# Stage seams of a two-layer encoder trunk worked by pairs of token tiles

## What is computed

```python
mod = (c_act @ w_ada[l] + b_ada[l])[:, None, :]
sh_a, sc_a, g_a, sh_m, sc_m, g_m = jnp.split(mod, 6, axis=-1)
h = x * (1.0 + sc_a) + sh_a
proj = h @ w_in[l]                      # heads of three attention mixers -> y
x = layer_norm(ALPHA * x + (1.0 + g_a) * (y @ w_o[l]), ln1_g[l], ln1_b[l])
h = x * (1.0 + sc_m) + sh_m
y = jnp.square(jax.nn.relu(h @ w1[l])) @ w2[l]
x = layer_norm(ALPHA * x + (1.0 + g_m) * y, ln2_g[l], ln2_b[l])
```

## Time and profile before

| | |
|---|---|
| median of three executions | 1447.26 us |
| the profiled execution | 1448.38 us |
| its span, first to last instruction | 1446.6 us |
| TensorE matmul busy | 1324.9 us (92%) |
| VectorE / ScalarE / GpSimd busy | 1011.6 / 598.5 / 339.9 us |
| granted TensorE clock, mean | 0.968 |
| DMA, mean | 114 GB/s |

### The profile page before, as it was taken

How to read it: one execution, slowest core, us unless ns; L and a number is a source line. 1 busy time by engine, 2 the same in 40 slices (tenths; PEclk the granted TensorE clock), 3 DMA queues, 4 the chain that set the end, 5 groups by cost and what they waited for, 6 DMA issues and landing times.

```text
span 1446.6 us, 19841 instructions
## 1 busy us (share of the span) xinstructions
PE 1324.9 (92%) x6696; PEld 1120.0 (77%) x6696; DVE 1011.6 (70%) x1650; ACT 598.5 (41%) x1212; POOL 339.9 (23%) x409
## 2 busy tenths in 40 slices
PE   4998998899899999999969899879989999999992
PEld 2897877787788888888869877768778888888882
DVE  6768788877678465565785878978674855454478
ACT  0356478851432222222244647878152232222221
POOL 0022066630125000000321406856010700000024
PEclk9999989999999999999989999999999999999996
DMA  8864600005233343344246462010423333333331
GB/s 284 302 203 165 204 14 14 27 22 173 76 119 128 117 129 113 100 129 147 79 154 202 155 212 72 1 39 1 145 87 96 95 99 97 94 98 98 95 102 58
DMA packets 87577, 164.38 MB, mean 114 GB/s; under 512 B 7960, under 2 KB 18584, under 8 KB 87504
## 3 DMA queue, kind: packets, MB, share of 16 engines
q1 hardware_dynamic: 86976, 161.34, 34.4%
q10 hardware_dynamic: 528, 2.10, 0.4%
HBM read 159.21 MB, written 4.19 MB: 113 GB/s over the span
## 4 chain that ended last, share of the span: by engine, by line
PE 68%; DVE 17%; DMA 6%; ACT 4%; issue 3%; POOL 2%; SPq 0%; ACTq 0%; DVEq 0%; POOLq 0%
PE bank L1325 21%; PE bank L1326 21%; PE bank L1327 21%; DMA ada_w<-in_w_ada 2%; DVE pt_lo L1076 2%; PE bank L1354 2%; DVE ada_sum L839 2%; PE bank L1492 2%; DMA slab_raw<-in_w_in 1%; DVE smax L1063 1%; DVE X L1104 1%; DVE stats L1107 1%; DVE tmp L1101 1%; DVE k_lo L1037 1%; DVE acc L1246 1%
## 5 line engine op out<-in xcount | busy, mean ns | idle before, releaser
L1325 PE MATMUL bank<-hT_hi,slab_hi 128*128 128x512 f32 x576 | 224.5, 390 | 1.2 <-ACT kB L658 1.2
L1156 DVE TENSOR_TENSOR slab_lo<-slab_raw,slab_hi 128x512 fp32r<-128x512 f32 x240 | 183.0, 815 | 60.1 <-ACT slab_hi L793 51.8
L1327 PE MATMUL bank<-hT_hi,slab_lo 128*128 128x512 f32 x576 | 224.1, 389 | 0.0
L1326 PE MATMUL bank<-hT_lo,slab_hi 128*128 128x512 f32 x576 | 224.1, 389 | 0.0
L1325 PE MATMUL bank<-slab_hi,h_hi 128*128 128x512 f32 x512 | 200.1, 391 | 2.8 <-ACT mod_a L810 2.8
L1327 PE MATMUL bank<-slab_hi,h_lo 128*128 128x512 f32 x512 | 199.3, 389 | 0.0
L1326 PE MATMUL bank<-slab_lo,h_hi 128*128 128x512 f32 x512 | 199.2, 389 | 0.0
L1325 PE MATMUL bank<-slab_hi,hT_hi 128*128 128x384 f32 (+3 forms) x448 | 151.6, 338 | 4.0 <-DVE hT_lo L1084 2.8
L1327 PE MATMUL bank<-slab_hi,hT_lo 128*128 128x384 f32 (+3 forms) x448 | 150.9, 337 | 0.0
L1326 PE MATMUL bank<-slab_lo,hT_hi 128*128 128x384 f32 (+3 forms) x448 | 150.8, 337 | 0.0
L839 DVE SCALAR_TENSOR_TENSOR ada_sum<-ada_w,c_col,ada_sum 128x512 f32<-128x512 f32 x168 | 129.5, 771 | 16.2 <-DMA ada_w<-in_w_ada 13.1
(11 more groups left out here) (198 smaller groups left out, 2601.2 us busy)
## 6 DMA issues: line engine op xcount, KB each, us to landing
slab_raw<-in_w SPq DMA_DIRECT2D x256, 256.0 KB, 2.7
ada_w<-in_w_ada SPq DMA_DIRECT2D x48, 1024.0 KB, 5.4
slab_raw<-in_w_in SPq DMA_DIRECT2D x48, 192.0 KB, 5.3
slab_raw<-in_w_o SPq DMA_DIRECT2D x32, 256.0 KB, 2.9
slab_raw<-in_w_in SPq DMA_DIRECT2D x16, 256.0 KB, 5.3
band<-bias_rows SPq DMA_DIRECT2D x8, 448.0 KB, 3.2
slab_raw<-in_w_in SPq DMA_DIRECT2D x16, 144.0 KB, 3.7
X<-in_x SPq DMA_DIRECT2D x1, 2048.0 KB, 10.1
```

The source lines that it names most:

```text
L1156: dve.tensor_tensor(slab_lo[:, slot, :], slab_raw[:, slot, :], f32(slab_hi[:, slot, :]), ALU.subtract).then_inc(slab_lo_done, 1)
L1325: pe.matmul(dst, a_hi, w_hi, start=first, stop=False)
L1326: pe.matmul(dst, a_hi, w_lo, start=False, stop=False)
L1327: return pe.matmul(dst, a_lo, w_hi, start=False, stop=last)
```

## The change

Tokens are handled in pairs of tiles, p = 0 (tiles 0, 1) and p = 1 (tiles 2, 3), at each seam.

- *Jobs and banks.* ln0 to ln3 become lnp, lnq (entry of a layer, pair 0 and 1) and lnr, lns (before the MLP). Each has eight pieces of 256 tokens, two to a bank. Banks come from a table (`SETS`, `EVEN`, `ODD`).
- *TensorE.* `wo_second` runs wo1 for pair 0, then pair 1, with pair 0's 16 transposes after slab 5 of pair 1. `first_group` runs W1's first group in two halves of 256 tokens, with pair 1's transposes around slab 7 of the first. `first_chunk` does the same for the first projection chunk. `last_group` leaves the W2 product of group 7 in the banks of group 6, pair 0 and then pair 1, and in layer 0 puts the next layer's first transposes between its slabs; in layer 1 tiles 2 and 3 come one after the other.
- *ScalarE* no longer normalises X. It evicts each piece once (256 tokens, `pair_tmp`), and VectorE casts and subtracts from that (`ht_low`).
- *GpSimd* normalises X with one subtract-and-multiply a half tile (`normalise`), so `shift` goes. It no longer takes part in the residual of the MLP.
- *VectorE.* `norm_exit` interleaves the residuals of tiles 2 and 3 with casts and splits. The gate and X are applied to `acc` (eight scalings, eight additions) before the squares of group 7; group 6 has no addition into `acc`.
- *Modulation.* The gate blocks 10 and 11 move to MLP groups 0 and 1 of each layer (`LATE`), a whole block a group; the next layer's blocks 0 to 3 are done in groups 2 to 5. "ad3" goes.
- *Output.* Eight stores of half tiles; GpSimd writes tiles 0 and 1, VectorE 2 and 3 (`last_affine`).
- *Memory.* Some SBUF tensors change their offsets; X, hT and the area of reused tensors start at multiples of 1024 bytes.

```diff
-        ("wo0", 0, 4), ("wo1", 0, 4), ("ad3", 2, 0), ("ln2", 4, 0), ("ln3", 4, 0), ("w1", 4, 0)]
+        ("wo0", 0, 4), ("wo1", 0, 4), ("lnr", 8, 0), ("lns", 8, 0), ("w1", 4, 0)]
...
+                def normalise(n):
+
+                    for t in range(TT):
+                        rstd_of(n, t)
+                        pool.wait_ge(rstd_ready, l * 8 + 4 * n + t + 1)
+                        for j in range(2):
+                            xs = X[:, t, 512 * j:512 * j + 512]
+                            pool.tensor_scalar(xs, xs, mv[:, t, MV_MEAN:MV_MEAN + 1], mv[:, t, MV_RSTD:MV_RSTD + 1],
+                                               ALU.subtract, ALU.mult).then_inc(xhat_ready, 1)
...
+                def ln_evac(job, which, k, l=l):
+                    p = int(job in ("lnq", "lns"))
+                    act.wait_ge(bank_ready, l * B_LAYER + ready_before(job) + k // 2 * 2 + 2)
...
+                    if 8 * p + k >= 4:
+                        act.wait_ge(ht_ready, l * 32 + which * 16 + 8 * p + k - 3)
+                    act.activation(pair_tmp(k), ln_bank(job, k), ACT.Identity, **move).then_inc(evac_act, 1)
+
+                def norm_entry(job, which, first, width, l=l):
+                    for k in range(4):
+                        split(first + k, width, l)
+                    ln_evac(job, which, 0, l)
+                    for k in range(4):
+                        ln_evac(job, which, k + 1, l)
+                        split(first + 4 + k, width, l)
+                    for k in range(5, 8):
+                        ln_evac(job, which, k, l)
...
+                def ht_low(job, k, l=l):
+                    p = int(job in ("lnq", "lns"))
+                    dve.wait_ge(evac_act, l * A_LAYER + a_before(job) + k + 1)
+                    step(dve.tensor_copy(hT_hi[:, k, pair_cols(p)], pair_tmp(k)))
+                    settle()
+                    dve.tensor_tensor(hT_lo[:, k, pair_cols(p)], pair_tmp(k), f32(hT_hi[:, k, pair_cols(p)]),
+                                      ALU.subtract).then_inc(ht_ready, 1)
...
+                def norm_exit(n, job, first, width, src, half_done, all_done, l_next):
+                    ht_low(job, 0, l_next)
+                    ht_low(job, 1, l_next)
+                    half_done()
+                    at2 = take(src(2), n, 2, 1)
+                    all_done()
+                    at3 = take(src(3), n, 3, 1)
+                    split(first + 4, width, l_next)
+                    ht_low(job, 2, l_next)
+                    add_to_x(n, 2, 1, at2)
+                    split(first + 5, width, l_next)
+                    stats_of(2, 1)
+                    add_to_x(n, 3, 1, at3)
+                    ht_low(job, 3, l_next)
+                    stats_of(3, 1)
+                    moments(2)
+                    split(first + 6, width, l_next)
+                    moments(3)
+                    ht_low(job, 4, l_next)
+                    split(first + 7, width, l_next)
+                    for k in range(5, 8):
+                        ht_low(job, k, l_next)
...
+                def first_group():
+                    def columns(p, ks, cs):
+                        for k in ks:
+                            pe.wait_ge(ht_ready, l * 32 + 16 + 8 * p + k + 1)
...
+                    columns(0, range(3), (0, 1))
+                    pe.wait_ge(evac_dve, l * D_LAYER + d_before("wo1") + 4)
+                    columns(0, range(3), (2, 3))
+                    columns(0, range(3, 7), range(4))
+                    transpose_x("lns", 1, range(4))
+                    columns(0, range(7, 8), range(4))
+                    transpose_x("lns", 1, range(4, 8))
+                    columns(1, range(8), range(4))
...
+                for j in range(2):
+                    for f in range(4):
+                        last_group((0, 1), j, f)
+                if l < DEPTH - 1:
+                    for f in range(4):
+                        last_group((2, 3), 0, f)
+                    for f in range(4):
+                        last_group((2, 3), 1, f)
+                        if f == 1:
+                            pe.wait_ge(evac_dve, l * D_LAYER + D_LAST + 4)
+                            transpose_x("lnp", 0, range(8), l + 1)
```

More of the change, by code:

```diff
@@ L490, in _ @@
                         affine_part(t, part, lnrow[:, 0, :], lnrow[:, 1, :])
[L492 to L510, removed]
@@ new lines, in _, with scale_acc @@
+                for k in range(4):
+                    split_at(k, base_at + (PRE + 16 + k + 1))
+                dve.wait_ge(x_ready, l * 8 + 8)
+                dve.wait_ge(evac_act, relu_base + 5 * LATE)
+                dve.wait_ge(evac_dve, l * D_LAYER + D_LAST)
+                gated[0] = D_LAST
+                def scale_acc(t, j):
+                    a = acc[:, t, 512 * j:512 * j + 512]
+                    step(dve.tensor_tensor(a, a, gate[:, 1, 512 * j:512 * j + 512], ALU.mult))
+                    return now()
@@ new lines, in base_of_x @@
+                def base_of_x(t, j, at):
+                    xs = X[:, t, 512 * j:512 * j + 512]
+                    dve.wait_ge(dve_step, at)
+                    step(dve.scalar_tensor_tensor(out=xs, in0=xs, scalar=ALPHA, in1=acc[:, t, 512 * j:512 * j + 512],
+                                                  op0=ALU.mult, op1=ALU.add))
+                for t in range(TT):
+                    at = [scale_acc(t, j) for j in range(2)]
+                    for j in range(2):
+                        base_of_x(t, j, at[j])
@@ new lines, in mlp_step @@
+                    pe.wait_ge(evac_act, relu_at + 4)
+                    if mod is not None:
+                        pe.wait_ge(ada_half, mod * 2 + 2)
+                        if wide:
+                            pe.matmul(h1_set[3][:, :], ones[:, :], ada_sum[:, 0, :], start=True, stop=True
+                                      ).then_inc(mod_ready, 1)
+                        else:
+                            mod_cols(h1_set[3], ada_sum[:, 0, :])
+                    w2_half(h1_set, gm, u, 1, at + (PRE + 20), None if mod is None else relu_at + 5, more)
@@ new lines, in _, with last_group @@
+                mlp_step(GROUPS - 2, 0, relu_base + 4 * (GROUPS - 2) + LATE + (AHEAD if l < DEPTH - 1 else 0), more=True)
+                def last_group(tiles, j, f):
+                    slot = 4 * j + f
+                    slab_ready(l * SLABS + SLABS - 8 + slot + 1)
+                    for t in tiles:
+                        ins = three(ff_bank(t, j)[:, :], h2_hi[:, 1, f, t * P:(t + 1) * P],
+                                    h2_lo[:, 1, f, t * P:(t + 1) * P], slab_hi[:, slot, :], slab_lo[:, slot, :],
+                                    False, f == 3)
+                        if f == 3 and j == 1 and tiles == (2, 3) and t == 2:
+                            ins.then_inc(ff_tile, 1)
+                    if tiles[-1] == 3:
+                        ins.then_inc(slab_free, 1)
+                    elif f == 3:
+                        ins.then_inc(ff_tile, 1)
```

630 lines of the change are left out of this document (347 added, 283 removed).

## The result

The changed kernel takes 1456.4 us (median of five executions, 1454.7 to 1458.8). The kernel before, run beside it, takes 1447.0. The ratio is 1.0061, with a 95% interval of 1.0048 to 1.0074: slower by 0.6%, where 1430.5 with a range of 1421 to 1442 was forecast. The profiled execution took 1457.35 us, its span 1455.6; the mean granted clock is 0.969 (before 0.968).

The account below looks back on a forecast made before the run. TensorE's matmul stream was taken as the bound, with VectorE the long chain inside seams. Terms 4.2 + 6.8 + 5.2 - 1.5 + 2.0 = 16.7 us off the profiled 1448.4 gave 1431.7; adjusted to the median, 1430.5, range 1421 to 1442.

Parts of the forecast that it names:

- between nothing and 0.72, their own length: Inner seams: bounds for what each of four late GpSimd normalising instructions costs VectorE; 0.6 us charged, 2.4 a seam.
- stalls about 0.5: Attention to MLP: TensorE waits about 0.5 us at the transposes inserted after six of wo1's eight slabs.
- the layer seam: From layer 0's last W1 block into layer 1's first projections: gain 7.8 us, 6.8 after late slabs.
- GpSimd's normalising by E + 42.6: Between layers: GpSimd has normalised tile 1 42.6 us after E, the end of the last W1 block.
- Rival C: TensorE's bursts through the first pair halve its clock in W1 and projections: 54 us lost, 1485; chance 0.06.
- the seam into the MLP: From attention's output to the end of W1's first group, in each layer: gain 4.4 us.
- the rest of layer 1's MLP: After W1's first group: gate block's all-ones matmuls cost 1.8 us, VectorE's extra products 0.5; together -2.3.
- the output end: From layer 1's last W1 block to the program's end: 65.3 us instead of 70.5, gain 5.2.
- The waits on mod_a: Modulation evictions ahead of slab splits in ScalarE's queue: TensorE's 2.8 us wait becomes about 0.8, +2.0.
- The new stall before W2's second half of group 6: Last groups of a layer: the first split comes late, TensorE stalls 2.3 us, 1.7 in layer 1.
- The entry: Start of layer 0: halving about even at -0.4, with late slots -1.5 us, bounds 0 and -5.
- Rival A: Three seams: VectorE beside GpSimd's normalising is the bound, 10 us less gain, 1440; chance 0.16.

Follow-up runs that it names:

- the one-factor form: The changed kernel with GpSimd's normalising in the inner seams as X times rstd times 1.0, the subtraction of the mean left out: 1423.1 us, ratio 0.9841.

## Why the prediction was wrong

**The step that failed** is in the seam from attention to the MLP: "GpSimd takes about 0.9 for the root (0.55 and a small one with its waits) and 2 x 0.72 for each tile". The 0.72 is that of a TENSOR_SCALAR with two multiplications. The new one subtracts, and the trace of before has no GpSimd TENSOR_SCALAR with a subtraction: its price had to be bounded from both sides, and the text took the nearest row as the value and as the upper bound ("between nothing and 0.72, their own length"). Measured: 2.20. Three of them stand before TensorE's wait, 3 x 1.5 = 4.4 us more of GpSimd's work in each pair. "Its normalised tile 1 is there at about 357.5" was 359.9 for the first half alone, and "stalls about 0.5" was 4.33. Not all of that is the subtraction: with multiply and add the same stall is still 2.25. From the root of tile 1 to its normalising GpSimd took 1.3 us in the change and 2.15 there, with the small instruction more, where 0.9 was charged. The same step stands in the layer seam ("GpSimd's normalising by E + 42.6").

**What came on top.** Rival C, the clock, had 0.06 and was set against a cause that didn't occur, bursts in the first pair. The clock fell for a plainer reason, at the new waits, and cost some 10 us. Its sign ("a granted clock of 0.50 that lasts into the second pair") came in another form: the clock is 1.00 again at 366 us and falls anew at the second pair's wait, as the windows at 382 and 384 show. A rival that joined a slow GpSimd to the clock behind its waits was missing, though the earlier trace rows show the clock at 0.50 right after one of the waits of the earlier trace rows, the 3.60 us before 366.58.

**What held.** With the operation swapped, the kernel took 1430.2 us against 1430.5 forecast. That is partly luck: in spans it gained 20.9 for 16.7, and its profiled execution is the quickest of its four. By stage, the seam into the MLP is +4.3 and +5.3 for 4.4; the rest of layer 1's MLP -1.8 for -2.3, the price of the gate block moved in; the output end +4.6 for 5.2; the layer seam +9.8 for 6.8, of which 1.6 is lost again up to wo0. In that seam 1.1 was a misreading: the last W1 block of the kernel before ends at 682.9, not at the 684.0 that was worked out, which left out the modulation's eight small matmuls (0.8). The waits on mod_a (2.8) went entirely, where 2.0 was expected. The new stall before W2's second half of group 6, forecast at 2.3, is 0.3 (row L1229): which part of that term was too dear was not separated. The entry was charged -1.5 and came even, though at its end 2 us could still be had from the order of the loads.

**Rival A**, VectorE with GpSimd at its side, is small. A cast on 256 takes 0.29 alone. Of the 17 that overlap a normalising instruction, six take 0.61 and eleven 0.28 to 0.30, nine of these with GpSimd at work from their start to their end: VectorE is not held for the whole length of each, as the 5.8 a seam would have it. Alone, one cast with its subtraction follows the other after 0.67 (0.68 charged); and TensorE waits 4.6 us for hT_lo in the whole span. The long cast of each layer, 3.52 us beside the memset of acc, held up nobody. VectorE's work makes GpSimd longer, too: the normalising takes 2.07 us at its shortest and 2.62 at its longest, the one-factor form 0.69 and 1.24.

The Trainium skill, "GPSIMD Engine Reference", section "3.1 Elementwise — side-by-side cycle accounting", gives 768 ns for a loop over 512 elements at best. The forms with one addition and one multiplication agree (762 to 930 ns). Two multiplications stay below it, 716 ns in attention and 0.69 us at the shortest in the seams; there the measurement decides. It gives no cost by operation, and the 2.08 to 2.22 us with subtract are measured here alone.

## What to carry to other kernels

Price an instruction by engine, kind, shape and operation; where the trace has no row with the same operation, the nearest row is a lower bound, and the range has to be as wide as the doubt. On GpSimd, (X - mean) * rstd is X * rstd + (-mean * rstd) with one tiny instruction for the constant, and that is 1.3 us less for each 128x512 (2.20 against 0.93). When a wait of a few us enters TensorE's stream, charge the half clock behind it as well (here some 10 us for 22.9 of waiting); an order that lets TensorE meet a slow producer is better mended at the producer than by filling (1422 against 1446).

## What the runs showed of the hardware

- GpSimd, 128x512 f32, TENSOR_SCALAR, mean of a group: multiply and multiply 0.72 to 0.87 us, multiply and add 0.76 to 0.93, add and multiply 0.89, subtract and multiply 2.08 to 2.34, multiply and subtract 2.22. With VectorE idle the subtracting form takes 2.08 (at 357.85 and 380.37 us); at the end of the program two of four take 2.58, beside VectorE's L1387 and L1390.
- A cast on 256 beside GpSimd's normalising takes 0.61 us in six cases and 0.28 to 0.30 in eleven. What parts the two was not tried.
- A wait of 2.25 us left TensorE's clock at 1.00; waits of 2.99 and 4.33 were followed by 0.50. Transposes of the identity, which nobody reads, kept it at 1.00 in the seams into the MLP.
